# A norm stage between two matmul stages: a weight split moved to GpSimd, transposed tiles dealt out anew, and the first two weight units multiplied together

## The reference, cut to what matters

```
x = layer_norm(ALPHA * x + f(x))      # mean and variance over the 1024 features
(xf - mu) * rsqrt(var + 1e-5) * g + b
```

```
gt, up = split(x @ w1, 2);  y = (silu(gt) * up) @ w2          # feed-forward
q, kv, ... = split_cols(h @ w_in)                              # token mixer
```

## Time and profile before

| | |
|---|---|
| median of 3 runs | 2810.22 us |
| the profiled execution's own time | 2808.6 us |
| its span in the profile | 2806.7 us |
| mean granted TensorE clock | 0.988 |
| PE busy | 2643.6 us |
| DVE busy | 1284.0 us |
| ACT busy | 1059.4 us |
| POOL busy | 68.9 us, 24 of its 28 instructions in L1102 |
| norm stages, by the start of L1007 | 204.2, 513.3, 709.1, 905.0, 1202.5, 1398.4, 1636.6, 2124.0, 2311.6 us |

### The profile page before, as it was taken

How to read it: one execution, slowest core, us unless ns; L and a number is a source line. 1 busy time by engine, 2 the same in 40 slices (tenths; PEclk the granted TensorE clock), 3 DMA queues, 4 the chain that set the end, 5 groups by cost and what they waited for, 6 DMA issues and landing times.

```text
span 2806.7 us, 40282 instructions
## 1 busy us (share of the span) xinstructions
PE 2643.6 (94%) x16574; PEld 1951.5 (70%) x16574; DVE 1284.0 (46%) x2355; ACT 1059.4 (38%) x1748; POOL 68.9 (2%) x28
## 2 busy tenths in 40 slices
PE   8999999999999999999989899989988999998996
PEld 8988988899898998889888754433336874443433
DVE  5565554755756565475677751111106653111112
ACT  4444563444444465344457641111113443111110
POOL 0001000100100100010010000000000000000000
PEclk9999999999999999999999999999999999999999
DMA  9636633565463853446353289999996339999997
GB/s 309 220 118 163 208 98 112 196 201 189 154 210 113 225 165 98 159 154 208 124 167 121 92 339 416 421 421 421 421 421 223 121 134 374 421 421 421 421 421 291
DMA packets 315366, 695.37 MB, mean 248 GB/s; under 512 B 58224, under 2 KB 243440, under 8 KB 266032
## 3 DMA queue, kind: packets, MB, share of 16 engines
q1 hardware_dynamic: 312000, 682.09, 66.1%
q10 hardware_dynamic: 3184, 10.69, 1.2%
HBM read 691.65 MB, written 1.08 MB: 247 GB/s over the span
## 4 chain that ended last, share of the span: by engine, by line
PE 66%; DMA 17%; DVE 9%; ACT 5%; issue 2%; SPq 1%; ACTq 0%; DVEq 0%
PE ps L295 26%; PE ps L2619 8%; PE ps L827 7%; DMA slots_over_xT<-in_moe_w_gate 6%; DMA ring<-in_moe_w_gate 6%; DMA moe_slots<-in_moe_w_gate 5%; PE ps L1605 4%; PE ps L2669 4%; PE ps L1645 3%; DVE weight_parts L226 3%; PE ps L334 2%; PE ps L306 2%; PE ps L2555 1%; ACT weight_parts L218 1%; PE ps L2636 1%
## 5 line engine op out<-in xcount | busy, mean ns | idle before, releaser
L295 PE MATMUL ps<-xT_upper,weight_parts 128*128 128x256 f32 (+1 forms) x4656 | 844.2, 285 | 17.7 <-DVE weight_parts L226 7.1
L226 DVE TENSOR_TENSOR weight_parts<-ring,weight_parts 128x1024 fp32r<-128x1024 f32 x479 | 612.0, 1281 | 491.5 <-ACT weight_parts L218 491.0
L295 PEld LDWEIGHTS ps<-xT_upper,weight_parts 128*128 128x128 f32 (+1 forms) x4656 | 718.5, 190 | 40.9 <-DVE weight_parts L226 13.7
L218 ACT ACTIVATE weight_parts<-ring 128x1024 fp32r<-128x1024 f32 x479 | 504.0, 1055 | 532.8 <-PE ps L295 320.3
L295 PE MATMUL ps<-xT_lower,weight_parts 128*128 128x256 f32 (+1 forms) x2328 | 650.9, 283 | 1.6 <-DVE xT_lower L988 1.5
L295 PEld LDWEIGHTS ps<-xT_lower,weight_parts 128*128 128x128 f32 (+1 forms) x2328 | 438.1, 190 | 3.4 <-DVE xT_lower L988 2.8
L2619 PE MATMUL ps<-ring,bias_tiles 128*64 128x512 f32 x1024 | 240.8, 595 | 24.1 <-DMA ring<-in_moe_w_gate 12.6
L2914 DVE TENSOR_TENSOR arena<-ps,arena 128x512 f32<-128x512 f32 x32 | 22.1, 692 | 468.4 <-ACT arena L2782 468.4
L827 PE MATMUL ps<-weight_parts,hidden_upper 128*128 128x512 f32 x704 | 218.5, 392 | 4.4 <-DVE hidden_lower L880 4.4
L2782 ACT ACTIVATE arena<-ps 128x512 f32<-128x512 f32 x32 | 19.1, 598 | 487.6 <-PE ps L2619 487.6
L2619 PEld LDWEIGHTS ps<-ring,bias_tiles 128*64 128x64 f32 x1024 | 78.0, 137 | 177.6 <-issue 127.0
(11 more groups left out here) (335 smaller groups left out, 3186.8 us busy)
## 6 DMA issues: line engine op xcount, KB each, us to landing
ring<-in_ffn_w SPq DMA_DIRECT2D x132, 1024.0 KB, 5.2
ring<-in_moe_w_up SPq DMA_DIRECT2D x64, 1024.0 KB, 26.4
ring<-in_moe_w_gate SPq DMA_DIRECT2D x64, 1024.0 KB, 26.2
ring<-in_moe_w_down SPq DMA_DIRECT2D x64, 1024.0 KB, 26.8
moe_slots<-in_moe_w_up SPq DMA_DIRECT2D x48, 1024.0 KB, 26.4
moe_slots<-in_moe_w_down SPq DMA_DIRECT2D x40, 1024.0 KB, 26.1
slots_over_xT<-in_moe_w_gate SPq DMA_DIRECT2D x32, 1024.0 KB, 27.2
moe_slots<-in_moe_w_gate SPq DMA_DIRECT2D x32, 1024.0 KB, 26.2
```

What stands on the lines that cost most here:

```text
L218: act.activation(self.part(n, 0), cut(self.stream.slot(pos)), ACT.Copy).then_inc(self.upper_done, 1)
L226: dve.tensor_tensor(self.part(n, 1), cut(self.stream.slot(pos)), self.part(n, 0).bitcast(F32), ALU.subtract).then_inc(self.split, 1)
L295: m = pe.matmul(out[0:rows, :], w[of_w][:, k, :], c.xTp[of_x][:, k, :], start=(at == 0), stop=(at == len(steps) - 1))
```

## The change

What it does:

1. GpSimd splits `lead[0]` (copy, then subtract) in a stream of its own, once PE is done with the unit whose place it takes; in router stages it splits the router weights. ACT and DVE no longer do. ACT's split of `lead[1]` waits for GpSimd's.
2. DVE's `sums` is cut into `added` and `statistics`, and `scales(0)` moves ahead of `statistics(1, 0)`.
3. The transposed tiles of t = 0 go to banks 4, 5 and 1, those of t = 1 to banks 2 and 3; PE transposes k = 4 to 7 first for t = 1, and signals every pair. `raw` is dealt out tile by tile: of t = 0 ACT takes k = 0, 1 and DVE 2 to 7; of t = 1 ACT takes 2, 3, 6, 7 and DVE 0, 1, 4, 5. ACT's first two tiles stand before and after its second square root, DVE's tile k = 2 ahead of `scales(1)`. The upper parts are made in the order (t0 h0), (t1 h0), (t0 h1), (t1 h1).
4. `first_products` takes the first two units of a stage together: all products with upper x of unit 0, then of unit 1, then those with lower x of unit 0, then of unit 1. It starts when the upper parts of k = 0 to 3 are there.
5. The zero products shrink from 512 to 256 columns ahead of t = 0 and from 1024 to 512 after both.

The diff, cut to its core (the two feed-forward-like callers of `first_products` in the mixer and the dilated attention are as in the hunk that is shown for the feed-forward; the setup stage's counts of `xT_hi` follow the new meaning):

```diff
@@ -48,7 +49,7 @@
 UNIT = SLOT // 2
 ARENA = 13856
 
-CLOCK_ROWS, CLOCK_PARTS, CLOCK_ROUTER = (512, 512), 1024, (1024, 2560, 512, 512)
+CLOCK_ROWS, CLOCK_PARTS, CLOCK_ROUTER = (256, 512), 512, (1024, 2560, 512, 512)
 CONSTANTS = 7 + 4 * DEPTH
 NORMS = 10
...
@@ -215,7 +216,9 @@
         self.stream.ready(act, pos)
         if n >= UNITS:
             act.wait_ge(self.done, n - UNITS + 1)
-        act.activation(self.part(n, 0), cut(self.stream.slot(pos)), ACT.Copy).then_inc(self.upper_done, 1)
+        into, src = self.part(n, 0), cut(self.stream.slot(pos))
+        ins = act.activation(into, src, ACT.Copy) if act.engine == ENGINE.Activation else act.tensor_copy(into, src)
+        ins.then_inc(self.upper_done, 1)
 
...
@@ -280,20 +283,42 @@
     return steps
 
 
-def feature_products(c, pe, n, out, fresh=False):
+def feature_products(c, pe, n, out):
 
 
 
     w = c.units.both(n)
     rows = c.units.all[n][2][1]
     pe.wait_ge(c.units.split, n + 1)
-    steps = by_arrival() if fresh else [(k, of) for k in range(KT) for of in PARTS]
-    for at, (k, (of_w, of_x)) in enumerate(steps):
-        if fresh and k % 4 == 0 and of_w == 0:
-            ready = (c.xT_hi, c.x_parts)[of_x]
-            pe.wait_ge(ready.sem, ready.at(k // 4 - 1))
-        m = pe.matmul(out[0:rows, :], w[of_w][:, k, :], c.xTp[of_x][:, k, :], start=(at == 0), stop=(at == len(steps) - 1))
+    for k in range(KT):
+        for of_w, of_x in PARTS:
+            m = pe.matmul(out[0:rows, :], w[of_w][:, k, :], c.xTp[of_x][:, k, :], start=(k == 0 and (of_w, of_x) == PARTS[0]),
+                          stop=(k == KT - 1 and (of_w, of_x) == PARTS[-1]))
     m.then_inc(c.units.done, 1)
+
+
+def first_products(c, pe, n, outs, one_bank):
+
+
+
+
+    def rounds(of_x, at):
+        w, rows = c.units.both(n + at), c.units.all[n + at][2][1]
+        for k in range(KT):
+            if at == 0 and k % 4 == 0:
+                ready, each = ((c.xT_hi, 2), (c.x_parts, 1))[of_x]
+                pe.wait_ge(ready.sem, ready.at(each * (k // 4 - 1)))
+            for of_w in range(2 - of_x):
+                m = pe.matmul(outs[at][0:rows, :], w[of_w][:, k, :], c.xTp[of_x][:, k, :],
+                              start=((of_x, k, of_w) == (0, 0, 0) and not (one_bank and at)),
+                              stop=(of_x == 1 and k == KT - 1 and not (one_bank and at == 0)))
+        return m
+
+    for at in range(2):
+        pe.wait_ge(c.units.split, n + at + 1)
+        rounds(0, at)
+    for at in range(2):
+        rounds(1, at).then_inc(c.units.done, 1)
...
@@ -813,8 +838,11 @@
                 m = 2 * n + half
                 if m >= 4:
                     pe.wait_ge(c.h_full.sem, c.h_full.at(m - 3))
-                for side in range(2):
-                    feature_products(c, pe, U[6 * n + 2 * half + side], ps[:, 4 + m % 4, side * S:(side + 1) * S], fresh=(m == 0 and side == 0))
+                outs = [ps[:, 4 + m % 4, side * S:(side + 1) * S] for side in range(2)]
+                if m == 0:
+                    first_products(c, pe, U[0], outs, True)
+                for side in range(2 if m else 0):
+                    feature_products(c, pe, U[6 * n + 2 * half + side], outs[side])
 
             def down(n, half, t, sides=(0, 1)):
...
@@ -914,8 +942,19 @@
     xT = c.xT_raw
     eps = c.tiny[:, 2:3] if weight == 1.0 else c.tiny[:, 3:4]
 
+    def turned(t, k):
+
+        bank = (4, 5, 1, 1)[k // 2] if t == 0 else 2 + k // 2 % 2
+        at = k % 4 if k >= 4 and t == 0 else 2 * (k // 4) * t + k % 2
+        return ps[:, bank, at * P:(at + 1) * P]
+
+    def arrived(t, k):
+
+        pair = k // 2
+        return (1, 2, 4, 4)[pair] if t == 0 else (7, 8, 7, 8)[pair]
+
     def out_of_psum(t, k):
-        return xT[:, k, t * P:(t + 1) * P], ps[:, 4 + 2 * t + k // 4, (k % 4) * P:(k % 4 + 1) * P]
+        return xT[:, k, t * P:(t + 1) * P], turned(t, k)
 
...
@@ -943,9 +982,11 @@
         def side(t, h):
             return c.x[:, t, h * 512:(h + 1) * 512]
 
-        def sums(t, h):
+        def added(t, h):
             dve.wait_ge(*done[t][h])
             ch.link(dve, dve.scalar_tensor_tensor(side(t, h), side(t, h), ALPHA / weight, ps[:, 2 * t + h, :], ALU.mult, ALU.add))
+
+        def statistics(t, h):
             ins = dve.bn_stats(stats[:, t, h, :], side(t, h))
             if h == 1:
...
         else:
-            sums(0, 0)
-            sums(0, 1)
-            sums(1, 0)
+            added(0, 0)
+            statistics(0, 0)
+            added(0, 1)
+            statistics(0, 1)
+            added(1, 0)
             scales(0)
-            sums(1, 1)
+            statistics(1, 0)
+            added(1, 1)
+            statistics(1, 1)
+            raw(0, (2,))
             scales(1)
             dve.tensor_scalar(side(1, 1), side(1, 1), mv[:, 1, 0:1], st[:, 1, 2:3], ALU.subtract, ALU.mult).then_inc(c.x_last.sem, c.x_last.one())
-            raw(0)
-            raw(1)
-            for n in lead[0:1]:
-                c.units.lower(dve, n)
-            if router:
-                dve.wait_ge(R.hi.sem, R.hi.at(1))
-                dve.tensor_tensor(c.router_parts[1], c.router_w[:, :], c.router_parts[0].bitcast(F32), ALU.subtract).then_inc(R.split.sem, R.split.one())
+            raw(0, (3,))
+            raw(1, (0, 1))
+            raw(0, (4, 5, 6, 7))
+            raw(1, (4, 5))
             for n in range(4):
                 lower(n)
             for n in lead[1:]:
                 c.units.lower(dve, n)
+
+    @block.gpsimd
+    def _(pool):
+        if lead:
+            if lent:
+
+                pool.wait_ge(*done[1][1])
+            pool.wait_ge(c.units.split, lead[0])
+            c.units.upper(pool, lead[0])
+            c.units.lower(pool, lead[0])
+        if router:
+
+            pool.wait_ge(c.units.done, c.units.limit)
+            pool.wait_ge(R.landed.sem, R.landed.issued)
+            pool.tensor_copy(c.router_parts[0], c.router_w[:, :]).then_inc(R.hi.sem, R.hi.one())
+            pool.wait_ge(R.hi.sem, R.hi.at(1))
+            pool.tensor_tensor(c.router_parts[1], c.router_w[:, :], c.router_parts[0].bitcast(F32), ALU.subtract).then_inc(R.split.sem, R.split.one())
...
-
-            act.wait_ge(c.xT_ps.sem, c.xT_ps.at(2 * t + 2))
-            for k in range(4, KT):
+        def raw(t, tiles):
+
+            act.wait_ge(c.xT_ps.sem, c.xT_ps.at(arrived(t, tiles[-1])))
+            for k in tiles:
                 dst, src = out_of_psum(t, k)
                 ins = act.activation(dst, src, ACT.Identity, scale=gT[:, k:k + 1], bias=gT[:, KT + k:KT + k + 1])
             ins.then_inc(c.xT_act.sem, c.xT_act.one())
 
-        def upper(n):
+        def upper(n, by_act, by_dve):
+
             t, h = n % 2, n // 2
-            sig = (c.xT_dve, c.xT_act)[h]
-            act.wait_ge(sig.sem, sig.at(t + 1))
+            if by_act:
+                act.wait_ge(c.xT_act.sem, c.xT_act.at(by_act))
+            if by_dve:
+                act.wait_ge(c.xT_dve.sem, c.xT_dve.at(by_dve))
             act.activation(half(c.xTp[0], t, h), half(xT, t, h), ACT.Copy).then_inc(c.xT_hi.sem, c.xT_hi.one())
 
         deviation(0)
         if not last:
-            if lent:
-
-                act.wait_ge(*done[1][1])
-            for n in lead[0:1]:
-                c.units.upper(act, n)
             normed(0)
-            if router:
-
-                act.wait_ge(c.units.done, c.units.limit)
-                act.wait_ge(R.landed.sem, R.landed.issued)
-                act.activation(c.router_parts[0], c.router_w[:, :], ACT.Copy).then_inc(R.hi.sem, R.hi.one())
+            raw(0, (0,))
         deviation(1)
         if not last:
+            raw(0, (1,))
             normed(1, (0,))
-            raw(0)
-            upper(0)
-            upper(2)
-            upper(1)
-            raw(1)
-            upper(3)
+            upper(0, 2, 2)
+            raw(1, (2, 3))
+            upper(1, 3, 3)
+            raw(1, (6, 7))
+            upper(2, 0, 4)
+            upper(3, 4, 5)
             for n in lead[1:]:
+
+                act.wait_ge(c.units.split, lead[0] + 1)
                 c.units.upper(act, n)
 
     @block.tensor
@@ -1073,14 +1129,13 @@
         if not last:
             for t in range(TT):
                 keep_clock(c, pe, CLOCK_ROWS[t])
-                for k in range(KT):
-
-                    if k % 4 == 0:
-                        ready = c.x_last.at(1) if t and k else c.x_new.at(2 * t + k // 4 + 1)
-                        pe.wait_ge((c.x_last if t and k else c.x_new).sem, ready)
-                    m = pe.transpose(ps[:, 4 + 2 * t + k // 4, (k % 4) * P:(k % 4 + 1) * P],
-                                     c.x[:, t, k * P:(k + 1) * P], c.ident[:, :])
-                    if k % 4 == 3:
+                for n, k in enumerate(range(KT) if t == 0 else (4, 5, 6, 7, 0, 1, 2, 3)):
+                    if n == 0 or (t == 0 and n == 4):
+                        pe.wait_ge(*((c.x_new.sem, c.x_new.at(1 + n // 4)) if t == 0 else (c.x_last.sem, c.x_last.at(1))))
```

(10 more changed lines are left out.)

30 lines of the change are left out of this document (17 added, 13 removed).

## The result

The kernel after takes 2817.07 us (median of 20 runs, 2812.78 to 2822.05), the kernel before 2811.72 (20 runs, 2808.88 to 2816.66). The ratio is 1.0015 with a 95% interval of 1.0009 to 1.0021: slower by 5.3 us in the medians and by 4.2 by the ratio (2.5 to 5.9), where 2809.3 was forecast and 2816.0 was the end of the range. The profiled execution took 2817.86 with a span of 2816.1, 9.4 more than the span before; single executions of one kernel scatter by 2 to 3 us (standard deviation), so the stages are read in the traces and the totals in the medians.

What follows compares the result with a forecast made beforehand. PE carries 66% of the chain, and norm stages are one serial string through DVE, ACT and PE. Reordering wins 5.2 us, GpSimd's holds lose 4.0 and 0.2: 1.0 won, 2809.3 us, range 2804 to 2816.

Steps and rivals of the forecast that it cites:

- C: Length of GpSimd's copy of a weight unit in the norm stages: taken as 1.3 us, bounds 1.06 and 2.35.
- 0.2 lost in both: Stages 2 and 5, behind mixers: the scaled mean L959 waits 0.1 for GpSimd's copy; 0.2 us lost together.
- rival 2: Stages 2 and 5: GpSimd's subtraction starts before L959 and holds it 2.2 us; 2812.4 in total, chance 0.12.
- rival 4: Idle stretches and fewer zero products drop PE's clock in five stages, 7.5 us lost; 2817 in total, chance 0.10.
- rival 3: GpSimd slow with strided or rounded output, its copy 2.35, holding L959 in six stages; 2815.5 in total, chance 0.15.
- Stages 1, 3, 4 and 6: The scaled mean L959 waits for GpSimd's copy, a delay of 1.0 us per stage; 4.0 us lost together.
- 0.6 won in each of stages 2 to 5: Reordering, GpSimd's cost aside: earlier upper parts let the first two units end at 718.9 instead of 719.5.
- 7.9: Stage 3: the fourth upper part, formerly there at 715.20 on the old trace's clock, comes at 714.1.
- The router's 1.2: Stages 7 and 9: ACT's L2763 and DVE's L2820 move up by 1.2 us; 1.2 won in each stage.
- The wait of 1.8 at the state-space stage: Behind stage 6 PE waits about 1.8 us at L2063 for dt's copy; still 0.3 us won.
- I take 0.1: Stage 8: shorter zero products save some, but unit 1 is split last with products still following; 0.1 us won.

Runs made afterwards that it cites:

- long zero products: Kernel after with zero products as long as before (512 and 1024 columns): 2816.41 us, ratio 1.0018.
- whole units: Kernel after with the first two units of a stage multiplied one after the other, as before: 2821.32 us, ratio 1.0030.
- GpSimd alone: Kernel before with only the first weight unit's split moved to GpSimd in six stages: 2818.15 us, ratio 1.0017.
- scaling back: Kernel after with the first scaling again behind the statistics, as before: 2817.47 us, ratio 1.0019.
- the reordering alone: Kernel before with only the new order inside the norm stage, plus the router's split on GpSimd: 2821.99 us, ratio 1.0037.
- one operand: Kernel after with the scaled mean written as a tensor_scalar with one tensor operand and a pointer: 2813.10 us, ratio 1.0000.
- no GpSimd: Kernel after with the first weight unit split on ACT and DVE again, the router's staying on GpSimd: 2814.45 us, ratio 1.0004.
- long ones in all stages but 8: Kernel after with one-operand scaled mean, whole units and earlier second scaling in stage 8, long zero products in the other stages: 2809.64 us, ratio 0.9990.
- short ones in stage 1 alone: Kernel before with zero products shortened (256 and 512 columns) only in stage 1: 2811.30 us, ratio 0.9998.
- Short zero products alone: Kernel before with only the zero products shortened to 256 and 512 columns: 2814.45 us, ratio 1.0009.

## Why the prediction was wrong

**The failed step.** "C isn't in the trace. Below it I put ACT's copy of that shape, 1.06", and from C = 1.3 "it waits 0.1: 0.2 lost in both" for stages 2 and 5. C is 1.04, 0.02 under my lower end, and below about 1.1 the subtraction begins before L959 is ready: rival 2, to which I gave 0.12. My own text had the threshold between my value and my bound, and I took the value away from it. The prediction's estimate from the Trainium skill ("GPSIMD Engine Reference", performance versus the Vector engine: a copy of about 1.1) was nearer to the measured 1.04 than my 1.3, and it lay on the threshold; its working isn't shown, and from the page's 1.03 cycles an element and 1.2 GHz the 1024 elements alone come to 0.88, also an estimate. The hold by the subtraction is 2.1 in each of the two stages, as rival 2 had it (2.2). The 2817 of rival 4 and the 2815.5 of rival 3 lie nearer to the result than the 2812.4 of rival 2, but by luck: the copy is 1.04 and not 2.35, and behind idle stretches of 0.8 the clock stayed up in stages 3, 4 and 5; it fell in stages 2 and 8, behind 3.4 and 1.55.

**What rival 2 didn't have** is the clock. PE's idle stretch of 3.4, which the hold makes, came before a low clock at the transposes in some stages: 1.7 more in stage 2 of the kernel after (third unit at 17.53, against 15.80 with the same hold and the clock up in the run with long zero products). Of the five traces with the hold it fell in none (long zero products), one (the kernel after) or both of the two stages (whole units, GpSimd alone, scaling back); of the twelve without it, in stage 2 of one (the reordering alone), and later in the stage. My rival 4 tied the fall to the shorter zero products in the stage; it happened with the long ones too (GpSimd alone).

**Stages 1, 3, 4 and 6.** Mechanism right, size off: with C at 1.04 L1000 lasts 0.6 longer, not 1.0, and the third unit comes 0.5 later (13.37 against 12.89), so about 2.0 for the four and not 4.0.

**The reordering.** "0.6 won in each of stages 2 to 5": stage 3 shows 0.41 with one operand and 0.52 with no GpSimd. With one operand the fourth upper part lets PE go on at 8.06 behind the first zero product, where I had 7.9, and L1000 itself is 0.05 longer. The router's 1.2 is exact at L2820 (8.91 to 7.70), but the experts' stretches of the table are only 0.9 and 0.3 shorter, where I had 1.2 each. The wait of 1.8 at the state-space stage is 1.86, and with one operand the stretch is level with before (238.11 against 238.16), where I had 0.3.

**Stage 8.** "I take 0.1": it lost 1.3 at the third unit (16.74 against 15.41). "Unit 1 is split last and its 16 plus 16 products must follow" is what I named and didn't price: the wait of 1.55 and the low clock behind it, which is 1.4 by itself (3.54 against 2.16 with one operand), as much as the stage lost. The tile copy ahead of the second scaling, which I overlooked, looks worse in the rows (the second L1000 at 2.62 behind the first zero product, before at 0.13 ahead of it) and cost nothing that the experiment shows.

**The sum.** The forecast counted from 2810.22, the median of three runs of the kernel before; over 20 runs it is 2811.72. So 1.5 of the 7.8 between forecast and result are the base, and 6.3 are the change (1.0 won in the forecast, 5.3 lost in the medians). The rows of one pair of traces give: stages 2 and 5, 2.05 each and one clock fall of 1.7, less the 0.2 priced, +5.6; the shorter hold in the four others, -2.0; the reordering, 0.2 less in each of four, +0.8; stage 8, +1.4; the router stages, +1.2; the state-space stage, +0.3. That is 7.3, 1.0 above the 6.3, which is within the scatter of a single execution. The falls of the clock in it (1.7 and 1.4) are those of this execution; what they are in the mean of the timed ones isn't known.

**What stays open.** The timed executions of the kernel after have a lower mean granted clock than those of the kernel before, by some 0.0025 (0.9849 against 0.9872 to 0.9878), and so, by 0.0008 or more, has every kernel with any part of the change but two (long ones in all stages but 8; short ones in stage 1 alone). A common slope, fitted within each kernel over the 293 timed executions, is 1.15 us for each 0.001, so this may be up to 3 us, the fall in stage 2 included. Short zero products alone cost 0.001 and 2.0 us in the means (2813.96 against 2811.95); long ones outside stage 8 bring 0.002 back but only 0.6 us. The falls that differ between the traces lie mostly in the stretches behind stages 1, 4 and 6, at other places in each execution, and no edit moved one of them reliably. So the zero products are a part of it by the clock, but how much of the time is theirs is not settled, and for the rest no experiment names a cause. The loss by the hold (4.0 in the medians, 6.8 from stage 2 to 7 of one pair of traces) is sure in its place, less so in its size. And with the hold gone the change still won nothing: the one-operand kernel's ratio is 1.0000.

## What to carry to other kernels

When GpSimd gets work beside VectorE, the unit of cost for a VectorE instruction with two SBUF operands is the whole instruction that GpSimd runs (here 0.16 became up to 2.31), and the question is which instruction will be running when the small one on the critical string comes up. Where a threshold lies between the value taken and its bound, both branches need a price and a fair chance. The cheapest cure here was to rewrite the small instruction so that it reads one tensor operand. And a reordering is judged by what its consumer wants first: here product order and tile order lost 7 and 10 us alone, and only together did they bring the third unit 0.4 to 0.5 forward.

## What the runs showed of the hardware

- A TENSOR_SCALAR with one tensor operand and one pointer operand in SBUF isn't held by GpSimd's subtraction or copy: 0.21 in the 11 of 18 cases that begin beside one, also 0.05 behind the subtraction's start, and the same in the five other kernels that have it. SCALAR_TENSOR_TENSOR on the same element lasts up to 0.78 in the copy's shadow and up to 2.31 in the subtraction's. By itself the TENSOR_SCALAR is slower: 0.21 against 0.16.
- GpSimd copies 128x1024 f32 to fp32r in 1.04, where ScalarE takes 1.06, and subtracts in 2.34 to 2.37, where VectorE takes 1.21. For 128x288 it takes 0.42 and 0.80. The gap between its two instructions, when they follow each other, is 0.08. A VectorE instruction that had begun before the copy's end got in; one that began 0.05 behind the subtraction's start was held to its end.
- After 3.42 of idle PE came back at the lower level in stage 2 and at the full one in stage 5, in the same execution of the kernel after (eight transposes in 1.97 and 1.36).
